# Up rows of tokens 0 to 255: from gathers to one pass over the table through an expert-by-token weight matrix

## The reference, cut to what matters

```python
def block(xb):
    ...
    g = jax.nn.softmax(fv, axis=-1)
    u = expert_down[eidx]
    act = jax.nn.gelu(jnp.einsum('thkd,td->thk', u, xb).astype(f32), approximate=False) * g
    v = expert_up[eidx]
    return jnp.einsum('thk,thkd->td', act.astype(v.dtype), v)
```

## Time and profile before

| | before |
|---|---|
| median of three runs | 2294.05 us (2289.31 to 2296.29) |
| profiled execution: span from the first to the last instruction | 2181.2 us |
| median less span: ahead of the first and behind the last instruction | 112.9 us |
| busy: PE, DVE, ACT, POOL | 1271.5, 1402.0, 428.4, 1060.0 us |
| moved by DMA | 696 MB, of which the gathers (queue q0) 545 MB |
| mean granted clock of PE | 0.765 |

### The profile page before, as it was taken

How to read it: one execution, slowest core, us unless ns; L and a number is a source line. 1 busy time by engine, 2 the same in 40 slices (tenths; PEclk the granted TensorE clock), 3 DMA queues, 4 the chain that set the end, 5 groups by cost and what they waited for, 6 DMA issues and landing times.

```text
span 2181.2 us, 20941 instructions
## 1 busy us (share of the span) xinstructions
PE 1271.5 (58%) x6676; PEld 757.3 (35%) x6676; DVE 1402.0 (64%) x3356; ACT 428.4 (20%) x901; POOL 1060.0 (49%) x1103
## 2 busy tenths in 40 slices
PE   5987898767668756368737575853223533222234
PEld 3854566654556434245414333531000100000000
DVE  3679991342677645378887667567767677767630
ACT  4112342301233311233320011211010101101000
POOL 1012221000336644347676566576757677767664
PEclk9889899788889877688868887986666655666556
DMA  9154464205779999899999999999989999999987
GB/s 294 48 182 166 136 213 138 79 9 215 255 278 394 396 401 321 318 324 405 403 404 400 397 387 405 394 383 409 410 326 410 383 410 410 409 410 409 403 348 284
DMA packets 260328, 696.11 MB, mean 319 GB/s; under 512 B 23743, under 2 KB 109847, under 8 KB 259119
## 3 DMA queue, kind: packets, MB, share of 16 engines
q0 software_dynamic: 149760, 545.33, 63.4%
q1 hardware_dynamic: 109346, 148.91, 20.3%
q10 hardware_dynamic: 1112, 0.53, 0.1%
HBM read 685.74 MB, written 9.08 MB: 319 GB/s over the span
## 4 chain that ended last, share of the span: by engine, by line
DMA 27%; POOL 12%; DVE 12%; PE 9%; issue 8%; ACT 2%; SPq 2%; DVEq 1%; POOLq 0%; ACTq 0%
DMA arena<-in_expert_up_dram,rows 15%; DMA arena<-in_expert_down_dram,expert 6%; POOL arena L1857 6%; POOL arena L1837 6%; DVE arena L2544 5%; DMA arena<-in_state_ssm_dram 5%; PE ps L2198 4%; PE ps L2230 2%; SPq L1699 1%; DVE arena L2591 1%; DMA arena<-in_w_branch_b_dram 1%; PE ps L2206 1%; DVEq L2485 1%; ACT arena L1903 1%; PE ps L2416 1%
## 5 line engine op out<-in xcount | busy, mean ns | idle before, releaser
L2544 DVE CUSTOM_DVE_ANT_0 arena<-arena,ps 128x1024 f32<-128x1024 f32 x512 | 610.3, 1219 | 246.2 <-DMA arena<-in_expert_down_dram,expert 236.1
L2198 PE MATMUL ps<-arena 128*32 128x512 f32 x2048 | 364.7, 846 | 604.8 <-DMA arena<-in_expert_up_dram,rows 597.0
L1837 POOL DMA_INDIRECT arena<-in_expert_down_dram,expert x512 | 491.4, 960 | 320.1 <-issue 139.8
L1857 POOL DMA_INDIRECT arena<-in_expert_up_dram,rows x512 | 487.5, 952 | 286.1 <-issue 147.6
L2230 PE MATMUL ps<-arena 128*128 128x264 f32 (+1 forms) x1344 | 344.5, 417 | 87.7 <-ACT arena L1933 31.6
L2198 PEld LDWEIGHTS ps<-arena 128*32 128x32 f32 x2048 | 74.8, 136 | 828.6 <-issue 819.9
L2230 PEld LDWEIGHTS ps<-arena 128*128 128x128 f32 x1344 | 273.8, 208 | 164.2 <-ACT arena L1933 33.7
L714 PE MATMUL ps<-arena 128*128 128x256 f32 x640 | 162.6, 411 | 3.5 <-ACT arena L544 3.5
L714 PEld LDWEIGHTS ps<-arena 128*128 128x128 f32 x640 | 128.7, 206 | 46.8 <-issue 27.3
L463 POOL TENSOR_TENSOR arena<-arena 128x512 f32<-128x512 f32 x16 | 23.1, 1442 | 243.2 <-DVE arena L1057 243.2
L1877 ACT ACTIVATE arena<-arena 128x8 f32<-128x8 f32 x65 | 13.5, 208 | 598.8 <-DVE arena L2544 598.5
(11 more groups left out here) (456 smaller groups left out, 1823.9 us busy)
## 6 DMA issues: line engine op xcount, KB each, us to landing
arena<-in_w_in_dram SPq DMA_DIRECT2D x42, 1024.0 KB, 8.2
arena<-in_w_ada_dram SPq DMA_DIRECT2D x32, 512.0 KB, 5.7
arena<-in_w_query_dram SPq DMA_DIRECT2D x16, 1024.0 KB, 17.4
arena<-in_w_ada_dram SPq DMA_DIRECT2D x8, 1024.0 KB, 19.5
arena<-in_w_ada_final_dram SPq DMA_DIRECT2D x16, 512.0 KB, 4.0
arena<-in_w_out_dram SPq DMA_DIRECT2D x8, 1024.0 KB, 18.5
arena<-in_expert_down_dram,expert POOLq DMA_INDIRECT x512, 12.2
arena<-in_expert_up_dram,rows POOLq DMA_INDIRECT x512, 11.9
```

What stands on the lines that cost most here:

```text
L1837: G.indirect_dma_start(U[i], None, down, bass.IndirectOffsetOnAxis(ap=at, axis=0))\
L1857: G.indirect_dma_start(Vr[r][j], None, up, bass.IndirectOffsetOnAxis(ap=at, axis=0))\
L2198: last = mm(ps[32 * j:32 * j + 32, c, :], Z[:, j, m, :], Vr[r][4 * half + j][:, c * 512:(c + 1) * 512], start=(p % 4 == 0 and m == 0), sto ...
L2544: V.tensor_tensor_reduce(U[i], U[i], row, 1.0, 0.0, ALU.mult, ALU.add, dots[n % 2][:, j:j + 1]).then_inc(s_uused, 1)
```

## The change

Tokens 0 to 255 (blocks 0 and 1, steps 0 to 31) keep their down gathers and lose their up gathers. Their 2 x 128 expert numbers and weights a token are kept (`EE`, `AC`), turned on PE and copied to `T3`, so that a column holds one token's 128 picks. An expert's number is row number times 128 plus column number. For four tokens at a time (a group, `k`, 256 groups), and for one of four spans of 32 of the 128 row numbers, POOL makes `AR` (128 picks x 32: the weight where the pick's row number is that of the place, L1955), ACT or DVE make `BR` (128 picks x 128: one where the column number is that of the place), and PE multiplies them, one product of 32 columns for each token (`build`, L2665). ACT copies what four groups give into `WT`, 128 column numbers x 32 row numbers x 256 tokens (`keep_wide`). Then SP reads the whole up table in 128 tiles of 128 experts (512 KB, plain loads, four buffers), and PE multiplies each tile by `WT` for both blocks and both halves of the row, four products of 512 columns a tile (`tile`, L2680), summed in four PSUM banks.

This runs in beats too, four a step from step 16 on (`next(dense)`). Groups 0 to 31 are built in beats 9 to 39, all of `BR` by ACT. Groups 32 to 255 are built four a beat, in beats 73 to 80, 81 to 96, 101 to 116 and 118 to 133 (steps 34 to 49), with `BR` by ACT and DVE in turn. Tiles come two a beat, in beats 84 to 99, 101 to 116, 119 to 134 and 137 to 152 (steps 37 to 54). `AR` and, from group 32 on, `BR` have four buffers each, that is one beat's groups.

Besides, the down ring is 8 deep, the samples' step stands ahead of unit 28 (step 56, before: step 40), blocks 0, 1, 2 and the samples are closed in units 28 to 31, three residual blocks are parked in DRAM for that time, and the products of blocks 2 and 3 read the token's row from SBUF where they read it from PSUM before.

```diff
--- before.py
+++ after.py
@@ -1483,6 +1483,10 @@
 GATE = 8
 LAG = 4
 VR = 8
+UR = 8
+WIDE_BLOCKS = 2
+WIDE = 32
+GT = 4
 
...
-    rows = [mem(Map.GB + j * D, D) for j in range(10)] + [mem(Map.HT + j * D, D) for j in range(4)]\
-        + [mem(Map.ROWS + j * D, D) for j in range(4)]
-    freed = [mem(Map.H2T + j * D, D) for j in range(2)]
+    U_rows = [mem(at + j * D, D) for at in (Map.HT, Map.ROWS) for j in range(4)]
+    V_rows = [mem(at, D) for at in (Map.KT, Map.KT + D, Map.RING, Map.RING + D, Map.KEEP, Map.KEEP + D,
+                                    Map.MG + Map.OTHER, Map.MG + Map.OTHER + D)]
+    tile_rows = [mem(at + j * D, D) for at in (Map.ZS + Map.OTHER, Map.CV + Map.OTHER + KD * HW) for j in range(2)]
+    WT_AT = (Map.GB, Map.SC + 4 * D - WIDE * 2 * P)
+    WT = [mem(at, WIDE, 2 * P) for at in WT_AT]
+    BR = [mem(at, GT, P) for at in (Map.GB + 8 * D, Map.GB + 8 * D + GT * P, Map.RING + 2 * D, Map.KEEP + 2 * D)]
+    AR = [mem(Map.GB + 9 * D + j * GT * WIDE, GT, WIDE) for j in range(4)]
+    T3 = [mem(Map.GB + 9 * D + 512 + b * 3 * P, 3, P) for b in range(2)]
...
-    units.insert(20, "samples")
+    units.insert(28, "samples")
...
+    def U_use(i):
+
+        return i % UR, 16 * (i // UR + 1)
...
-    at_step = {n: [n - LAG] for n in range(LAG, NSTEP)}
+    at_step = {n: [n - LAG] for n in range(LAG, NSTEP) if n - LAG in up_at}
...
+    close_at = {units.index(u): c for u, c in ((28, 0), (29, 1), (30, 2), (31, NB))}
     closings = [close_at[u] for u in sorted(close_at)] + [NB - 1]
...
+    NTILE = NK
+    NGROUP = NK // WIDE * 2 * P // GT
+    PER = NGROUP * WIDE // NK
+
+    def group(k):
+
+        return k // PER, k % PER // (P // GT), GT * (k % (P // GT))
+
+    def slot(k):
+
+        return k % 2 if k < PER // 2 else k % 4
+
+    def by_vector(k):
+
+        return k >= PER // 2 and k % 2 == 1
+
+    def group_bank(k):
+
+        return k // 4 % 2 if k < PER else 4
+
+    def make_beat(k):
+
+        if k < PER // 2:
+            return 8 + k
+        if k < PER:
+            return 72 + (k - PER // 2) // 4
+        return (80, 100, 117)[k // PER - 1] + k % PER // 4
+
+    def tile_beat(i):
+
+        return (84, 101, 119, 137)[i // WIDE] + i % WIDE // 2
+
+    BEATS = 153
...
 
...
-            sp.wait_ge(t_ss, 1)
-            for dst, m in ((gate, 5), (shift, 6), (scale, 7)):
-                sp.dma_start(dst[:, 0, :], mod_d[NS:NC_ROWS, m * D:(m + 1) * D].partition_broadcast(P)).then_inc(s_rows, 16)
...
+            for i in range(NTILE):
+                if i >= len(tile_rows):
+                    sp.wait_ge(s_used, i - len(tile_rows) + 1)
+                if i == 3 * WIDE + len(tile_rows):
...
+                sp.dma_start(tile_rows[i % len(tile_rows)], up[i * P:(i + 1) * P, :]).then_inc(s_tile[i % len(tile_rows)], 16)
+            sp.wait_ge(s_used, NTILE)
+            for c, at in enumerate((0, P, 3 * P, 4 * P, 5 * P)):
+                n = P if c < NB else NS
+                sp.dma_start(x_in[c], keep_d[at:at + n, :]).then_inc(s_x1a, 16)
...
+                for k in range(NGROUP):
+                    yield from until(make_beat(k) + 4)
+                    c, b, t0 = group(k)
...
+                    if k >= 4:
+                        pool.wait_ge(s_group, k - 3)
+                    for t in range(GT):
+                        at = t0 + t
+                        one = G.tensor_scalar(AR[k % 4][:, t, :], iota_e[:, WIDE * c:WIDE * (c + 1)], T3[b][:, 0, at:at + 1],
+                                              T3[b][:, 2, at:at + 1], ALU.is_equal, ALU.mult)
+                    one.then_inc(s_A, 1)
+
+            late = wide()
             for n in range(NSTEP):
+                some = n >= PH * 2 and steps[n] != S
                 gather_down(n)
+                if some:
+                    next(late, None)
+                    next(late, None)
                 for m in at_step.get(n, ()):
                     gather_up(m)
+                if some:
+                    next(late, None)
 
         @block.scalar
...
+                def one_hot(k):
...
+                    for t in range(GT):
+                        one = SE.activation(BR[slot(k)][:, t, :], iota_e, ACT.Square, bias=T3[b][:, 1, t0 + t:t0 + t + 1],
+                                            scale=-1.0)
+                    one.then_inc(s_square, 1)
+                    squares += 1
+                    act.wait_ge(s_square, squares)
+                    SE.activation(BR[slot(k)], BR[slot(k)], ACT.Relu, bias=ones[:, 0:1], scale=-1.0).then_inc(s_BS, 1)
+
+                def keep_wide(k):
+
+                    c, b, t0 = group(k)
+                    act.wait_ge(s_group, k + 4)
...
+                    if c >= 2 and k % PER == 0:
+                        act.wait_ge(s_used, WIDE * (c - 1))
+                    src = ps[:, group_bank(k), :].rearrange("p (t i) -> p i t", i=WIDE)
+                    SE.activation(WT[c % 2][:, :, P * b + t0:P * b + t0 + 4 * GT], src, ACT.Copy).then_inc(s_WT, 1)
...
+                    for k in made_at(beat - 2):
+                        if k % 4 == 3:
+                            keep_wide(k - 3)
+                    for k in made_at(beat):
+                        if not by_vector(k):
+                            one_hot(k)
...
+                def build(k):
+
+                    if by_vector(k):
+                        pe.wait_ge(s_BV, sum(by_vector(j) for j in range(k + 1)))
+                    else:
+                        pe.wait_ge(s_BS, sum(not by_vector(j) for j in range(k + 1)))
+                    pe.wait_ge(s_A, k + 1)
+                    if k % 4 == 0 and k >= 8:
+                        pe.wait_ge(s_WT, k // 4 - (k < PER))
...
+                    for t in range(GT):
+                        at = (k % 4 * GT + t) * WIDE
+                        last = mm(ps[:, group_bank(k), at:at + WIDE], BR[slot(k)][:, t, :], AR[k % 4][:, t, :],
+                                  start=True, stop=True)
+                    last.then_inc(s_group, 1)
...
+                def tile(i):
+
+                    c = i // WIDE
+                    if i % WIDE == 0:
+                        pe.wait_ge(s_WT, PER // 4 * (c + 1))
+                    if i == 0:
+                        pe.wait_ge(s_xs, 2)
...
+                    pe.wait_ge(s_tile[i % len(tile_rows)], 16 * (i // len(tile_rows) + 1))
+                    for b in range(2):
+                        for h in range(2):
+                            last = mm(ps[:, (2, 6)[b] + h, :], WT[c % 2][:, i % WIDE, P * b:P * (b + 1)],
+                                      tile_rows[i % len(tile_rows)][:, 512 * h:512 * h + 512], start=(i == 0), stop=(i == NTILE - 1))
+                    last.then_inc(s_used, 1)
...
+                    for k in made_at(beat - 1):
+                        build(k)
+                    for i in range(NTILE):
+                        if tile_beat(i) == beat:
+                            tile(i)
...
+                for half in range(2):
+                    if g != S:
+                        for _ in range(2):
+                            next(late, None)
+                            if n >= 2 * PH:
+                                next(dense, None)
+                    if n - LAG in up_at:
+                        add(n - LAG, half)
...
             def products(n):
 
-                row = xs if steps[n] == S else hb
+                row = xs if steps[n] == S else token_row[steps[n] // (2 * PH)]
...
+                def one_hot(k):
+
+                    c, b, t0 = group(k)
+                    if slot_free(k):
+                        dve.wait_ge(s_group, slot_free(k))
...
+                    tt(BR[slot(k)], iota_e.unsqueeze(1).to_broadcast([P, GT, P]),
+                       T3[b][:, 1, t0:t0 + GT].unsqueeze(2).to_broadcast([P, GT, P]), ALU.is_equal).then_inc(s_BV, 1)
```

More of the change, by code:

```diff
@@ L1503, in stage_peer @@
     Z = take(4, 8, 32)
+    EE = [mem(Map.Z + b * 2 * P, 2, P) for b in range(2)]
+    AC = [mem(Map.Z + 4 * P + b * P, P) for b in range(2)]
     sel = take(2 * PH, NS, rows=NS)
@@ L1596, in stage_peer @@
[L1596 to L1602 removed]
+    Vr = [V_rows, U_rows]
@@ L1604, in stage_peer, with made_at, slot_free @@
+    def tile_beat(i):
+        return (84, 101, 119, 137)[i // WIDE] + i % WIDE // 2
+    BEATS = 153
+    def made_at(beat):
+        return [k for k in range(NGROUP) if make_beat(k) == beat]
+    def slot_free(k):
+        before = [j for j in range(k) if slot(j) == slot(k)]
+        return before[-1] + 1 if before else None
     halves = [(c, hh) for c in (2, 3) for hh in range(2)]
@@ L2773, in front, with wide, until, beats @@
                 V.memset(Q.qpad, 0.0).then_inc(t_zero, 1)
-            late = front()
+            def wide():
+                now = 0
+                def until(beat):
+                    nonlocal now
+                    assert beat >= now, (beat, now)
+                    while now < beat:
+                        now += 1
+                        yield
```

(27 more changed lines are left out.)

304 lines of the change are left out of this document (198 added, 106 removed).

## The result

| | us (median) | span of the profiled execution |
|---|---|---|
| before | 2291.7 (2282.9 to 2296.3, 4 runs) | 2181.2 |
| after | 2735.4 (2727.8 to 2737.2, 4 runs) | 2735.5 |

The ratio is 1.193, 95% interval 1.190 to 1.197: slower by 444 us. The forecast was 2630 us, range 2460 to 2790, with 0.60 on 2500 to 2700: the measured time lies in the range, outside that inner band, and beside the 2740 of rival (b).

What follows compares the result with a forecast made beforehand. Bytes and POOL's issuing bound the second half before; PE was to become the bound in the dense steps. 2181.2 - 152 + 487 = 2516 us of span, plus 113 outside it, gave 2630 us, range 2460 to 2790.

Steps and rivals of the forecast that it cites:

- rival (b): Steps 34 to 54: POOL becomes the bound, AR dearer than 0.4 us; loss 597 us, total 2740 us; chance 0.20.
- Steps 0 to 33: First part, with up gathers of steps 4 to 31 removed: 736 us instead of 888, a gain of 152.
- Covered: Building 32 early groups, in 10 steps: PE's 31 us and ACT's 32 x 2 us fit in idle time.
- AR at 0.25 us: POOL's AR instruction (128x32), steps with builds: 0.25 us each, 64 make 16 us, POOL 36 us a step.
- PE's 46.8 us a full step: Full steps within 34 to 54: builds 15.4, tiles 27.5, add 3.84 us at full clock, making PE the bound.
- The stand of 6 us: Full steps: PE waits 6 us for the first group's AR, queued on POOL behind four gathers.
- Steps 34 to 36: Steps that build without tiles: POOL sets them, 10 + 16, 10 + 16, 20 + 16 = 88 us.
- Steps 40, 41, 45, 49 and 50 to 54: Partial steps 167 us; step 50 28 by DMA; steps 51 to 53 102; step 54 23.
- Step 55 to the end: Tail, 16 gathers a step again: 0 to 5 us more for parked rows and moved loads, taken as 0.
- 113 us outside the span: Whole run: 113 us lie outside the profiled span and are added to 2516 us, giving 2629.
- The price of a product: Tile products of 512 columns on PE: 0.43 us a record, 0.86 a product, 3.44 a tile, 128 tiles 440.
- (c): Rival for the dense steps, its sign full steps near 31 us; chance 0.05.

Runs made afterwards that it cites:

- e1: Changed kernel without AR, BR, builds, WT copies, tiles and their loads, so only the removal of 256 up gathers is left: 2028.1 us, ratio 0.929.
- e3: Changed kernel with the last beat of AR in a POOL step put ahead of that step's up gathers, nothing left out: 2690.1 us, ratio 1.231.
- e2: Changed kernel with one AR instruction a group of four tokens instead of four (three tokens' weights not made): 2598.7 us, ratio 1.189.
- e7: Changed kernel with tile products of 128 columns instead of 512, all loads, builds and AR kept: 2633.6 us, ratio 1.145.
- e8: Changed kernel with AR made by DVE instead of POOL and tile products of 128 columns instead of 512: 2377.3 us, ratio 1.037.
- e5: Changed kernel with AR made by DVE, two 128x128 instructions a group, instead of four on POOL; nothing left out: 2536.2 us, ratio 1.104.
- e9: Changed kernel with AR by DVE, 128-column tile products and one 128-column build product a group instead of four of 32: 2267.5 us, ratio 0.989.
- e0: Kernel before, unchanged, profiled and timed again: 2182.6 us, ratio 0.999, span 2189.7 us for an execution of 2191.4.

## Why the prediction came out as it did

The direction and the place were right: DMA falls to 0.58, PE works the most, a stand for AR comes once a step, the loss is in steps 34 to 54. The bound was half right: POOL stands as a second one beside PE, which was rival (b), given 0.20, and its sign (L1955 above 0.4 us) is what came. The number, 2630 for 2735, is 4% low, and it is that near only by luck: a sum that was 220 us low had a false 113 added. By the prediction's steps:

**Steps 0 to 33, 736 forecast, 775 measured.** The lighter gathers alone give 735 (e1), but by two misses that cancel. Of the 85 us that DVE waited for states in steps 4 to 15 I left 8; after still has 44.7 of them, since ACT waits for the state's load:

```profile
ACT arena L2012 <- DMA arena<-in_state_ssm_dram: 71.5, 5, 21.2
DVE arena L2866 <- ACT arena L2012: 44.7, 4, 16.4
```

So taking away the up gathers halves the wait for the states and doesn't end it; that step failed by 28 us, and steps 16 to 33 gave them back. What holds up the loads that still come late was not tried. "Covered" for the 32 early groups was wrong: they cost 30 us on one chip (e3 765 against e1 735), and 10 more are after's other chip or AR's place. 12 of the 30 are POOL's AR, or its place (steps 16 to 33: 375 in e3, 363 in e2); PE's and ACT's part of the other 18 was not taken apart.

**AR at 0.25 us: the mis-sized term.** Its rows in the timeline show 15.30 us for 32 instructions, 0.48 each (median of all 1024: 0.46, mean 0.51); it lay between the bounds named, 0.14 and 0.87, but at twice the value taken. The choice between the neighbours went by the size of the output; a TENSOR_SCALAR of 128x32 costs more than a select of 128x128 (0.29), so size was the wrong guide. This is rival (b): 31 us of AR beside 20 of gathers. Its sum of 34 to 54 is 1049 against 1084 measured, with the three steps ahead at 136 (163 measured) and a full one at 65 (61.4). Its total, 2740, is luck as well: it too holds the false 113, and without it would be 2626.

**PE's 46.8 us a full step.** At the full clock its parts are as forecast: two tiles 7.11 us (forecast 6.9), 16 tokens 3.65 (3.84), an add 3.84. The six steps hold 23 beats of builds and 22 of tiles, by these prices 44 us of PE a step; measured are 53.2. The 9 us between are the lower clock. Summed over the timeline, some 6 of them lie right behind the stand (builds 7.4 us instead of 3.65, tiles 9.5 to 9.8 instead of 7.11) and 3 to 4 elsewhere, mostly behind the other half of the add, where PE had waited 1.3 us at most (builds 3.8 to 7.1, tiles 8.7 to 9.5). So a stand is not the only thing that costs the clock here. The forecast took the middle between two clocks, and e2, with AR cheap, has 56.2 for a full step where it said 59.

**The stand of 6 us.** Confirmed in e2 (6.02). In after PE's idle time is 9.3 us a step. What was missed is that the waits go round: POOL's own chain of 47.8 busy + 4.2 + 10.4 waiting is 62.4 us, PE's of 53.2 + 9.3 is 62.5. Neither engine is full, and halving the load of either gives only a part (e2, e7), both together more than the sum (e8).

**Steps 34 to 36, 88 forecast, 163 measured.** The largest single miss, 75 us. On like chips it comes apart: with no AR on POOL these steps take 119 us (e5), so AR's price is 44; with one build product a group 92 (e9) where the same kernel with four had 116 (e8), so the small products are 24; what is left is within 4 us of the forecast. The small products were the term put at nothing, on the ground that POOL sets these steps: PE has no tiles here, works in short pieces at a granted clock of 0.54 (0.56 in e5), and is busy 102 of e5's 119 us.

**Steps 40, 41, 45, 49 and 50 to 54, 320 forecast, 369 measured.** In the first four it is the same AR and clock as in the full ones (201 for 167). Steps 50 to 54 have neither AR nor builds, and take 168 us for 153 on both kinds of chip (after, e2, e3); with narrow tiles they take 151 to 156 (e7, e8, e9, slow chips), so the rest is the tiles on PE and not the bytes.

**Step 55 to the end, 0 to 5 us more forecast.** On the quick chip 277 to 279 us against 258: 20 more. Also in e1, so it is not the dense work but what else the change holds: the shorter ring, the closings together, the parked rows, or products that read SBUF and slow POOL's gathers (1.02 us each in e1's tail, 0.94 in before's). Which of them was not tried.

**"113 us outside the span".** False (e0: 1.7). The sum is 2181 - 152 + 487 = 2516 on the chip of the profile. The terms above, -2 + 39 + 145 + 38 = 220, fill the whole distance to 2736, some of it (17 us in the last stretch) probably the slower chip.

**DVE beside POOL.** Neither the forecast nor the sum of rival (b) has a price for this. In e3 POOL makes 16 AR in 7.24 us where DVE is idle, and in 12.19 where DVE makes two BR and four products of two SBUF rows (here one of the four):

```profile
1862.87 7.24 POOL L1955 TENSOR_SCALAR arena<-arena 128x32 f32<-128x32 f32 x16
...
1883.93 12.19 POOL L1955 TENSOR_SCALAR arena<-arena 128x32 f32<-128x32 f32 x16 [3.88 <-PE ps L2665]
```

```profile
1887.15 1.22 DVE L2801 CUSTOM_DVE_ANT_0 arena<-arena 128x1024 f32<-128x1024 f32 x1
```

12.19 - 7.24 is 4.95 us. One AR beside a BR of DVE took 0.97 us; two more, beside a BR and the four products (1886.54 to 1891.80, 5.26 us), took 3.02 and 2.39 instead of 0.46 each. POOL lost 4.5 of these 5.26 us, nearly their whole length. But most products fall on POOL's gathers or waits, and a gather is lengthened less (in e3 and in after up to 1.99 us, median 0.94). Over 1818 to 2193 L1955 averages 0.505 us against an undisturbed 0.46, and the down gathers 1.21 us against 0.94 (eight a step): 2.8 + 2.2 us a step.

```profile
L1955 POOL TENSOR_SCALAR arena<-arena 128x32 f32<-128x32 f32 x368 | 181.2, 505 | 0.7
L1903 POOL DMA_INDIRECT arena<-in_expert_down_dram,expert x49 | 59.3, 1211 | 13.3 <-issue 13.2
```

**The price of a product.** 16 records of 512 columns in 7.11 us at clock 1.00 are eight products of 0.89 us, 0.44 a record; the forecast took 0.86 and 0.43 from rows of before. Full steps near 31 us, the sign of (c), came in no run with all of PE's work (51.5 us in e5, the shortest of these), and with 18.7 us of PE a step in e9 (31.2).

## What to carry to other kernels

Replacing a gather by a dense product trades bytes, which were full, for work on engines that only looked free: price every small instruction that makes the operands (here 1024 of 0.48 us and 1024 products with weights of their own), not only the large product. Where two engines at 85% and 76% each wait once a round for the other, the round is longer than the work of either (62.5 us for 53 and 52); test it by taking load off both, since either alone gives little. And before a difference between span and median is added as a term, look whether the two numbers come from the same chip.
